# Attention values with V stationary and the weights moving: two heads on two column halves of TensorE, weights scaled before their transposes

## The reference, cut to what matters

```
mixer a, per head:  s = q k^T * R, masked to a causal window;  m = max(max(s), sink)
                    p = exp(s - m) / (sum(exp(s - m)) + exp(sink - m));  o = p v
                    result = (o * silu(z)) @ w_out
mixer b, per head:  o = g0 * attn(q, k_cmp, v_cmp) + g1 * attn(q, k_sel, v_sel) + g2 * attn(q, k_win, v_win)
                    g0..g2 = sigmoid gates;  result = (o * silu(z)) @ w_out
silu(z) = z * sigmoid(z), here 0.5 * z * (1 + tanh(z / 2))
```

## Time and profile before

| | us |
|---|---|
| time, median of 3 runs (lowest, highest) | 2304.29 (2303.45, 2306.67) |
| profiled execution: its own time | 2302.39 |
| profiled execution: span, first to last instruction | 2301.1 |

### The profile page before, as it was taken

The page is one execution under the profiler, slowest core; times in us unless marked ns, Lnnn a source line. Parts: engine busy times, 40 slices in busy tenths (PEclk is TensorE's granted clock), DMA queues, the critical chain, the costliest instruction groups (busy, mean ns, idle before and its releaser), DMA issues.

```text
span 2301.1 us, 27346 instructions
## 1 busy us (share of the span) xinstructions
PE 2225.4 (97%) x10723; PEld 1828.8 (79%) x10723; DVE 1462.9 (64%) x1847; ACT 1075.9 (47%) x1573; POOL 178.0 (8%) x318
## 2 busy tenths in 40 slices
PE   5888999999998999999999999999999999999997
PEld 5776888888877888888888888888888877877786
DVE  5768877888884666566445456666655536666664
ACT  3233456544436443543443454555554524565553
POOL 0004211122220100010000000100000000000000
PEclk9889999999999999999999999999999989999999
DMA  9987856688884777777565555544445634333233
GB/s 346 334 300 246 286 176 226 220 297 303 311 294 158 244 232 241 228 235 228 180 197 188 189 192 184 184 145 144 144 150 187 217 114 129 108 110 124 98 128 128
DMA packets 242164, 468.53 MB, mean 204 GB/s; under 512 B 14362, under 2 KB 52468, under 8 KB 241396
## 3 DMA queue, kind: packets, MB, share of 16 engines
q1 hardware_dynamic: 213840, 388.79, 51.5%
q0 software_dynamic: 20480, 67.13, 8.6%
q10 hardware_dynamic: 7716, 10.88, 1.4%
HBM read 464.65 MB, written 2.10 MB: 203 GB/s over the span
## 4 chain that ended last, share of the span: by engine, by line
PE 88%; DVE 5%; DMA 2%; issue 2%; ACT 1%; POOL 1%; SPq 1%; ACTq 0%; DVEq 0%
PE banks L612 26%; PE banks L614 25%; PE banks L613 25%; PE banks L623 2%; DMA ada_w<-in_w_ada 2%; PE banks L899 2%; PE banks L911 1%; DVE ada_acc_vec L1668 1%; DVE ada_acc L1629 1%; PE banks L926 1%; PE banks L925 1%; PE banks L924 1%; PE banks L993 1%; SPq L457 1%; ACT w_high L1122 1%
## 5 line engine op out<-in xcount | busy, mean ns | idle before, releaser
L1609 DVE TENSOR_TENSOR w_low<-raw,w_high 128x1024 fp32r<-128x1024 f32 x674 | 821.6, 1224 | 622.2 <-ACT w_high L1122 621.0
L1122 ACT CAST w_high<-raw 128x1024 fp32r<-128x1024 f32 x674 | 701.6, 1046 | 842.3 <-PE banks L614 842.3
L612 PE MATMUL banks<-w_high,act_a_high 128*128 128x512 f32 (+1 forms) x1696 | 693.6, 409 | 17.0 <-DVE act_a_low L1701 13.5
L613 PE MATMUL banks<-w_low,act_a_high 128*128 128x512 f32 (+1 forms) x1696 | 669.0, 394 | 0.0
L614 PE MATMUL banks<-w_high,act_a_low 128*128 128x512 f32 (+1 forms) x1696 | 668.9, 394 | 0.0
L612 PEld LDWEIGHTS banks<-w_high,act_a_high 128*128 128x128 f32 x1696 | 327.7, 193 | 97.5 <-issue 21.0
L614 PEld LDWEIGHTS banks<-w_high,act_a_low 128*128 128x128 f32 x1696 | 326.9, 193 | 69.9
L613 PEld LDWEIGHTS banks<-w_low,act_a_high 128*128 128x128 f32 x1696 | 327.3, 193 | 63.8 <-issue 2.4
L612 PE MATMUL banks<-w_high,act_b_high 128*128 128x512 f32 x640 | 252.2, 394 | 0.5 <-DVE o_chunk L1884 0.5
L614 PE MATMUL banks<-w_high,act_b_low 128*128 128x512 f32 x640 | 250.4, 391 | 0.0
L613 PE MATMUL banks<-w_low,act_b_high 128*128 128x512 f32 x640 | 250.3, 391 | 0.0
(11 more groups left out here) (326 smaller groups left out, 2096.1 us busy)
## 6 DMA issues: line engine op xcount, KB each, us to landing
raw<-in_w_ff SPq DMA_DIRECT2D x128, 1024.0 KB, 5.2
raw<-in_w_in SPq DMA_DIRECT2D x64, 1024.0 KB, 7.0
ada_w<-in_w_ada POOLq DMA_DIRECT2D x256, 256.0 KB, 4.4
raw<-in_b_w_in SPq DMA_DIRECT2D x44, 1024.0 KB, 5.0
raw<-in_a_w_in SPq DMA_DIRECT2D x36, 1024.0 KB, 5.1
ada_first<-in_w_ada SPq DMA_DIRECT2D x64, 512.0 KB, 9.0
raw<-in_w_o SPq DMA_DIRECT2D x16, 1024.0 KB, 7.1
raw<-in_a_w_out SPq DMA_DIRECT2D x16, 1024.0 KB, 5.1
```

What stands on the lines that cost most here:

```text
L612: T.matmul(out, xh, wh, start=(c.first and k == 0), stop=False)
L613: T.matmul(out, xh, wl, start=False, stop=False)
L1122: A.copy(WH[:, h % SPL, :, :], split_ap(h)).then_inc(*done("high", h))
L1609: V.tensor_tensor(WL[:, h % SPL, :, :], split_ap(h), WH[:, h % SPL, :, :].bitcast(F32), ALU.subtract).then_inc(*done("low", h))
```

## The change

The values become the stationary operand and the transposed weights move. Each head's output comes out transposed (64 rows of v's width by 256 tokens) and lands in one half of PSUM's partitions, so the two heads of a pair occupy the two column halves of the array: for each head 256 columns of weights move against v of the first 128 tokens, then 128 columns against v of the second. Since tokens are now along the free dimension, whatever is a factor per token has to be applied to the weights before their transposes: DVE multiplies the exponentials in place by the reciprocal row sum (times the branch gate in b, times `rh`), in `pair_scale`, called from `sink_scale` and `gate_scale` four steps after the scores; `pair_turn` now waits for `weights_scaled` instead of `scores_exp`. In a the sink arithmetic is done for each pair rather than for two.

The pairs of b are reordered so that both branches of two heads follow each other (branch = i % 2), and both branches and the compressed one accumulate in the same PSUM bank: `cmp_values` at rel 12 becomes four matmuls of 256 columns, one at the first pair of each two heads. z is transposed (`z_turn` at rel 18 and 21, four blocks each, stored by ACT in `z_store`), and the product with z is made on the transposed output (`out_gate`, DVE), cast (`out_high`, ACT) and subtracted (`out_low`, DVE) for every two heads. `oo`, `oo_turn`, `oo_gate`, the scaling of outputs and the branch additions are gone. Some small operations are new: a reciprocal of `rh`, and the gates of b times `rh`. The core of the diff:

```diff
+BRANCHES = {"a": 1, "b": 2}
+Z_STEPS = (18, 21)
...
+def gate_step(name, j):
+
+    return max(value_step(name, BRANCHES[name] * (j + 1) - 1) + 1, Z_STEPS[1])
...
-            T.wait_ge(*of("scores_exp", (name, g, i)))
+            T.wait_ge(*of("weights_scaled", (name, g, i)))
...
         def pair_values(name, g, i, vals):
-            if i % 2 == 0:
+            j, first, last = i // BRANCHES[name], i % BRANCHES[name] == 0, (i + 1) % BRANCHES[name] == 0
+            if first:
                 T.wait_ge(*emptied[3])
+            if first and name == "b":
+                T.wait_ge(*of("cpt_made", g))
+                T.matmul(bank(3)[:, 0:SEQ], vbd[0:HB, g, j * P:(j + 1) * P], cpt[0:HB, :, :].rearrange("p a n -> p (a n)"),
+                         start=True, stop=False)
             T.wait_ge(*of("pt_made", (name, g, i)))
             v0, v1 = (vals[:, tt, g * HD:(g + 1) * HD] for tt in range(2))
             for e in range(2):
-                s, c0 = 2 * (i % 2) + 1 - e, (2 * (i % 2) + e) * HD
-                o0, o1 = bank(3)[:, c0:c0 + HD], bank(3)[:, SEQ + c0:SEQ + c0 + HD]
-                T.matmul(o0, pt[:, s, 0:P], v0, start=True, stop=True)
-                T.matmul(o1, pt[:, s, P:2 * P], v0, start=True, stop=False)
-                mm = T.matmul(o1, pt[:, s, 2 * P:3 * P], v1, start=False, stop=True)
+                T.matmul(bank(3)[e * HD:(e + 1) * HD, 0:SEQ], v0, pt[:, 2 * (i % 2) + 1 - e, 0:SEQ],
+                         start=(name == "a"), stop=False)
+            for e in range(2):
+                mm = T.matmul(bank(3)[e * HD:(e + 1) * HD, P:SEQ], v1, pt[:, 2 * (i % 2) + 1 - e, 2 * P:3 * P],
+                              start=False, stop=last)
             mm.then_inc(*done("valued", (name, g, i)))
-            if i % 2 == 1:
-                emptied[3] = of("outputs_read", (name, g, i // 2))
-
-        def oo_turn(name, g):
-            for half in range(2):
-                T.wait_ge(*of("oo_gated", (name, g, half)))
-                turn_half("oo_" + name, g, oo, half, 2)
+            if last:
+                emptied[3] = of("out_gated", (name, g, j))
+
+        def z_turn(name, g, half):
+            T.wait_ge(*of("pair_free", (name + "_z", g)))
+            transposes(2, zs, 2 * half * P).then_inc(*done("z_turned", (name, g, half)))
+            emptied[2] = of("z_stored", (name, g, half))
...
+            if rel in Z_STEPS:
+                z_turn(name, g, Z_STEPS.index(rel))
...
-        def cmp_values(g):
-            for b in (2, 3):
-                T.wait_ge(*emptied[b])
-            T.wait_ge(*of("cpt_made", g))
-            for tt in range(NT):
-                mm = T.matmul(bank(2 + tt), cpt[0:HB, tt, :], vbd[0:HB, g, :], start=True, stop=True)
-            mm.then_inc(*done("cmp_valued", g))
...
+        def z_store(name, g, half):
+            if g > 0 and half == 0:
+                A.wait_ge(*of("out_gated", (name, g - 1, GH // 2 - 1)))
+            A.wait_ge(*of("z_turned", (name, g, half)))
+            A.copy(zT[:, 2 * half:2 * half + 2, :], two(bank(2))).then_inc(*done("z_stored", (name, g, half)))
+
+        def out_high(name, g, j, H):
+            A.wait_ge(*of("out_gated", (name, g, j)))
+            A.copy(H[:, GH // 2 * g + j, :], gated[:, j % 2, :]).then_inc(*done("out_high", (name, g, j)))
+
         def pair_hooks(name, g, rel, H):
-            if rel == OO_STEP[name]:
-                turn_high("oo_" + name, g, H, 4 * g, 2)
+            for j in range(GH // 2):
+                if rel == gate_step(name, j):
+                    out_high(name, g, j, H)
...
+        def pair_scale(name, g, i, factor):
+
+            s = 2 * (i % 2)
             for tt in range(NT):
-                V.scalar_tensor_tensor(out=oo[:, tt, cols], in0=oo[:, tt, cols], scalar=rh[:, tt:tt + 1], in1=zs[:, tt, cols],
-                                       op0=ALU.mult, op1=ALU.mult).then_inc(*done("oo_gated", (name, g, half)))
-
-        def half_heads(ap):
-
-            return ap.rearrange("p (a h d) -> p a h d", a=NT, d=HD)
+                c0, n = (0, P) if tt == 0 else (P, SEQ)
+                w = sc[:, s:s + 2, c0:c0 + n]
+                V.tensor_tensor(w, w, factor[:, :, tt].unsqueeze(2).broadcast_to([P, 2, n]),
+                                ALU.mult).then_inc(*done("weights_scaled", (name, g, i)))
+
+        def out_gate(name, g, j):
+            V.wait_ge(*of("valued", (name, g, BRANCHES[name] * (j + 1) - 1)))
+            V.wait_ge(*of("z_stored", (name, g, j // 2)))
+            if g > 0 or j >= 2:
+                V.wait_ge(*of("out_low", (name, g, j - 2) if j >= 2 else (name, g - 1, j + 2)))
+            V.tensor_tensor(gated[:, j % 2, :], bank(3)[:, 0:SEQ], zT[:, j, :],
+                            ALU.mult).then_inc(*done("out_gated", (name, g, j)))
+
+        def out_low(name, g, j, H, L):
+            V.wait_ge(*of("out_high", (name, g, j)))
+            k = GH // 2 * g + j
+            V.tensor_tensor(L[:, k, :], gated[:, j % 2, :], H[:, k, :].bitcast(F32),
+                            ALU.subtract).then_inc(*done("out_low", (name, g, j)))
+
+        def out_hooks(name, g, rel, H, L):
+            for j in range(GH // 2):
+                if rel == gate_step(name, j):
+                    out_gate(name, g, j)
+                if rel == gate_step(name, j) + 1:
+                    out_low(name, g, j, H, L)
...
+        def sink_scale(g, i):
+            hs = slice(2 * i, 2 * i + 2)
+            V.wait_ge(*of("sink_exp", (g, i)))
+            V.tensor_tensor(rd[:, hs, :], rd[:, hs, :], sm[:, 0, hs, :], ALU.add).then_inc(*done("rd_step", ("a", g, i, 0)))
+            V.wait_ge(*of("rd_step", ("a", g, i, 0)))
+            V.tensor_tensor(rd[:, hs, :], rd[:, hs, :], rh_inv.unsqueeze(1).broadcast_to([P, 2, NT]),
+                            ALU.mult).then_inc(*done("rd_step", ("a", g, i, 1)))
+            V.wait_ge(*of("rd_step", ("a", g, i, 1)))
+            V.reciprocal(rd[:, hs, :], rd[:, hs, :]).then_inc(*done("rd_step", ("a", g, i, 2)))
+            V.wait_ge(*of("rd_step", ("a", g, i, 2)))
+            pair_scale("a", g, i, rd[:, hs, :])
...
+                    if rel == score_step("a", i) + 4:
+                        sink_scale(g, i)
...
+        def gate_scale(g, i):
+            br, j = i % 2, 2 * (i // 2)
+            hs, g0 = slice(j, j + 2), 32 * (br + 1) + GH * g + j
+            V.wait_ge(*of("scores_exp", ("b", g, i)))
+            V.reciprocal(rd[:, hs, :], sm[:, br, hs, :]).then_inc(*done("rd_step", ("b", g, i, 0)))
+            V.wait_ge(*of("rd_step", ("b", g, i, 0)))
+            V.tensor_tensor(rd[:, hs, :], rd[:, hs, :], gts[:, :, g0:g0 + 2].rearrange("p a h -> p h a"),
+                            ALU.mult).then_inc(*done("rd_step", ("b", g, i, 1)))
+            V.wait_ge(*of("rd_step", ("b", g, i, 1)))
+            pair_scale("b", g, i, rd[:, hs, :])
...
+                    if rel == score_step("b", i) + 4:
+                        gate_scale(g, i)
```

More of the change, by code:

```diff
@@ L47 @@
                  "cols_made", "cols_copied", "bias_made", "c_tanh", "x_squared", "xn_made", "row_copied", "xT_made", "ident_made"),
-    "columns": ("mod1_sum", "mod1_made", "mod2_sum", "mod2_made", "sinks_made", "sinks_group", "sink_less", "square_sums",
+    "columns": ("half_inverse", "mod1_sum", "mod1_made", "mod2_sum", "mod2_made", "sinks_made", "sinks_group", "sink_less", "square_sums",
                 "heads_sums", "sink_exp"),
@@ L60 @@
     "cmp": ("cmp_scored", "cmp_turned", "cmp_valued", "cmp_exp", "cpt_made", "cmp_masked", "cmp_step", "cmp_shifted",
-            "cmp_weighted", "oo_begun"),
-    "outputs": ("outputs_read", "branch_added", "rd_step", "oo_gated"),
+            "cmp_weighted"),
+    "outputs": ("rd_step", "weights_scaled", "z_turned", "z_stored", "out_gated", "out_high", "out_low"),
     "pair": ("pair_free", "f_gated", "x_added", "gated", "sg_merged", "squared", "heads_squared", "z_tanh"),
@@ L1425, in pair_exp @@
             A.wait_ge(*of("minus_max", (name, g, i)))
+            br = i % BRANCHES[name]
             for e in range(2):
-                j, s = 2 * (i % 4) + e, 2 * (i % 2) + e
+                j, s = 2 * (i // BRANCHES[name]) + e, 2 * (i % 2) + e
                 for tt in range(NT):
                     c0, n = (0, P) if tt == 0 else (P, SEQ)
-                    A.activation(sc[:, s, c0:c0 + n], sc[:, s, c0:c0 + n], ACT.Exp, scale=R, bias=nm[:, i // 4, j, tt:tt + 1],
-                                 accum_out=sm[:, i // 4, j, tt:tt + 1]).then_inc(*done("scores_exp", (name, g, i)))
+                    A.activation(sc[:, s, c0:c0 + n], sc[:, s, c0:c0 + n], ACT.Exp, scale=R, bias=nm[:, br, j, tt:tt + 1],
+                                 accum_out=sm[:, br, j, tt:tt + 1]).then_inc(*done("scores_exp", (name, g, i)))
         def before(name, g, i):
@@ L1455, in pair_hooks @@
                     pair_exp(name, g, i)
+            if rel in Z_STEPS:
+                z_store(name, g, Z_STEPS.index(rel))
         def silu(name, g):
@@ L1490, in scalar_program @@
```

(26 more changed lines are left out.)

96 lines of the change are left out of this document (20 added, 76 removed).

## The result

The changed kernel takes 2404.76 us (median of 4 runs, 2402.82 to 2407.48) against 2303.87 of the kernel before on the same chip: ratio 1.0441, 95% interval 1.0421 to 1.0461. The profiled execution has a span of 2402.9 us, 101.8 more than before.

A forecast was written before the change was run, and what follows sets the result against it. It took PE, busy 97% of the span, as the bound, with DVE's scaling newly on its path; +60 in b, +23 in a and +17 for the clock made +100 on 2302.4, forecast 2404 us, range 2345 to 2440.

The forecast's parts named there:

- The wait and its price: Transposes in b wait for DVE's scaling: 9.2 us between turns against 7.21, +2.0 for 20 intervals, 40 us.
- Mixer a: Waits before a's transposes: 1.2, 3.0, 2.4, 1.2 us, 7.8 per group; +5.8 after savings, four groups +23.
- Turn 6 to 7: Late in each group of b: +4.9 us in the first three groups, 14.7 together; +1.6 in the last.
- The values' visit: PE's values' product per pair: column halves overlap, 1.06 us against 1.35; 48 pairs, -14 us.
- The clock: One in four of 48 new PE waits followed by 3.4 us at half clock: +17 us, ends 0 and +45.
- Turn 0 to 1: First interval of each group of b: 7.8 us against 5.9, +1.9 four times, 7.6.
- turn 7 to the next scores: After b's last transposes in a group: -1.07 us three times, -3.2; the last group's end counted separately.
- The sum: Whole kernel: b +60, a +23, clock +17, together +100 us on 2302.4; 2404 as median.
- The end: Behind b's last turn: shorter visits, no `oo` transposes, no 1.6 us wait for act_d_low: -2.7 us.
- In time: Rival: weights scaled before PE arrives, only PE's savings left, about -19 us, 2285; chance 0.07.

The follow-up runs named there:

- half_scale: Changed kernel with the second of the scaling's two multiplications (512 elements, second 128 tokens) left out: 2366.91 us, 37.8 under the changed kernel.
- early_both: Changed kernel with the scaling two instead of four steps after its scores, in both mixers: 2293.97 us, ratio 0.9964 to the kernel before.
- wait_only: Kernel before plus only the wait: DVE multiplies the exponentials by one four steps after the scores, transposes wait for it: 2441.01 us, ratio 1.0602.
- scale_early_old: Kernel before with DVE's multiplication by one and the wait for it, two steps after the scores: 2312.39 us, ratio 1.0043.
- early_zfirst: Changed kernel with scaling two steps after the scores in both mixers, and ACT's z_store ahead of out_high: 2282.66 us, ratio 0.9912.
- wait_only_look: Kernel before with the wait and multiplication by one four steps after the scores, run again for its profile: one execution of 2445.48 us.

## Why the prediction was right, step by step

The forecast was 2404 and +100; measured 2404.76 and +101. The steps:

- **The wait and its price**: 9.2 us forecast for every interval of turns 1 to 6, 9.24 to 9.30 measured wherever the clock stayed up (14 of 20; the other 6, after half-clock stretches, read 9.84 to 9.89). The wait is for DVE's work: `half_scale` shortens the interval by what it takes from DVE, `early_both` removes the wait, `wait_only` brings it without the rest of the change, and `scale_early_old`, with the same work and the same semaphore two steps earlier, costs 10 us. This is shown. Inside an interval DVE keeps the times of the forecast: counted from the turn at 2106.65, the mask starts at 4.13 (forecast 4.1), w_low at 6.24 (6.2), out_low at 7.38 (7.4), the scaling's last result comes at 9.15 and the next turn at 9.29 (9.2):

```profile
2110.78 0.96 DVE L2041 TENSOR_TENSOR scores<-banks,mask_causal 128x768 f32<-128x768 f32 x1 [2.01 <-PE banks L907]
...
2112.89 1.22 DVE L1624 TENSOR_TENSOR w_low<-raw,w_high 128x1024 fp32r<-128x1024 f32 x1
2114.03 0.42 DVE L2079 TENSOR_TENSOR act_d_low<-ada_acc,act_d_high 128x256 fp32r<-128x256 f32 x1
...
2114.77 1.03 DVE L2065 TENSOR_TENSOR scores<-scores,row_rec 128x256 f32<-128x256 f32 x2
```

- **Mixer a**: 1.2, 3.0, 2.4 and 1.2 forecast per group; from scores to turn 7.80, 7.84, 7.84, 7.81 became 9.05, 10.85, 10.29 (once 10.47), 9.06: +1.25, +3.01, +2.45, +1.25.
- **Turn 6 to 7**: 11.0 forecast from the chain rotation, out_gate, out_high, cast, w_low, out_low, scaling; measured 10.84, and 7.78 in the last group (forecast 7.7). PE waited 4.89 there, the longest of its waits before transposes. The chain is in the timelines of DVE and ACT, against the earlier trace rows:

```profile
2131.45 0.42 DVE L2019 TENSOR_TENSOR qr<-qr,rope_tmp 128x256 f32<-128x256 f32 x1
2131.79 0.42 DVE L2073 TENSOR_TENSOR ada_acc<-banks,z_transposed 128x256 f32<-128x256 f32 x1
2133.62 1.23 DVE L1624 TENSOR_TENSOR w_low<-raw,w_high 128x1024 fp32r<-128x1024 f32 x1 [1.42 <-ACT w_high L1123]
2134.76 0.42 DVE L2079 TENSOR_TENSOR act_d_low<-ada_acc,act_d_high 128x256 fp32r<-128x256 f32 x1
...
2132.24 0.40 ACT L1453 CAST act_d_high<-ada_acc 128x256 fp32r<-128x256 f32 x1 [1.82 <-DVE ada_acc L2073]
2132.55 1.04 ACT L1123 CAST w_high<-raw 128x1024 fp32r<-128x1024 f32 x1
```

- **The values' visit**: 1.06 forecast, 1.01 measured. Small, and in b it hid in the wait.
- **The clock**: near in size, with a wrong rule behind it. I took one wait in four, alike. In the profile of after all 11 waits of 2.75 us or more are followed by a stretch at 0.50, and 6 of the 37 shorter ones (three of about 1.9 and three of 2.25): 17 stretches where I took 12. A stretch costs where PE's work comes next on the path. Turn 0 to 1 was forecast at 7.8 and reads 9.25 to 9.27, because the transposes' record is 1.51 instead of 0.85 and the first tile takes 2.3 instead of 1.4: 5.8 us in four groups. In a it falls between the second turn and the next scores, 4.59 to 5.78 us where `early_zfirst` has 3.14: 7.2 us. The six intervals of 9.84 to 9.89 cost 3.8 over the 9.24 of the same places in the first group. Behind the three longest waits, from turn 7 to the next scores, PE takes 15.8 us where `early_zfirst`, with the same work, has 14.45: 4.0. That makes 21 in all against the 17; since the kernel before has one such stretch there too (1.6 us), the change adds 19.
- **The sum**: the total is closer than its terms. In a the waits and visits came to 25.0 us (forecast 23), the clock to 19.2 (17), and turn 7 to the next scores, without the clock, to -5.3 (-3.2). Two terms came out 2 us too small and one 2 us too large; that they cancel in part is luck. The other terms lie within 0.8 us. Counted another way, PE's idle time grew from 75.7 to 162.4 us; the time at clock 0.50 grew from 104.0 to 160.5, which is 28 us of busy time; and of PE's own work about 13 us are gone (an estimate, what is left of its busy time), near the -14 of the forecast.
- **The end**: -2.7 forecast behind the last turn, -2.6 measured.
- **In time** (the faster rival): 2285 forecast for the case that the weights are scaled before PE arrives. That case was built: 2293.97 with the early scaling alone, 2282.66 once z is stored first, which the forecast did not see as a second condition.

PE's transposes after one of the longest of these waits:

```profile
2136.68 1.51 PE L919 MATMUL banks<-ident,scores 128*128 128x128 f32 x6 [4.89 <-DVE scores L2065]
```

and the busy time of PE, PEld, DVE, ACT and POOL in two stretches, then PEclk, against the earlier trace rows:

```profile
2164.40:2167.10 2.70, 2.51 (x9) 2.34 (x10) 1.18 (x2) 0.96 (x2) 0.00 (x0) 0.50 0.21 22
2167.20:2170.40 3.20, 3.20 (x19) 2.21 (x18) 1.36 (x3) 2.44 (x9) 0.00 (x0) 0.99 0.83 307
```

The first stretch follows the 2.77 us wait before turn 0 of the third group: nine matmul records in 2.70 us, where the next has nineteen in 3.20.

## What to carry to other kernels

When an operation moves ahead of a wait, write down the program of the engine that gets it, between the event that feeds it and the one that needs it: one and a half microseconds for each of 48 pairs, on an engine that is 64% busy, made a change that saves PE work cost 101 us. Two steps earlier the same work cost at most 10 (`scale_early_old`), and the change gained 10. Shares of busy time say nothing of this; the timeline does, by the distance between the event that feeds the operation and the one that needs it. And in each engine's step, put first what another engine waits for (z's store), and last what itself waits (the cast of the gated output).

## What the runs showed of the hardware

Column halves of TensorE overlap in fp32 as row halves do: eight passes that need 1.31 us on the whole array took 1.01, the entry and exit of the mode included. Stretches at clock 0.50 follow short silences of TensorE: in the profile of after, every one of 11 waits of at least 2.75 us before transposes and 6 of 37 between 0.3 and 2.3 us. They come without a silence too: the one of the kernel before follows a visit of 32 matmuls of 15 columns. And a kernel that lets PE wait pays more than its waits: 86.6 us more of idle time came with 28 us more of work at half the clock in the changed kernel, and 87.3 with 57 in `wait_only_look`.
